# Moving the splits of the first weight slices around the conditioning, with their loads on GpSimd's queue

## The chip, the cores and the metric

One core of a Trainium2 chip. The metric is the time of one execution on the device in microseconds (us), the median of several. Engines: TensorE (PE; PEld is its weight load), VectorE (DVE), ScalarE (ACT), GpSimd (POOL) and SyncE (SP), which only issues transfers here. L461 is line 461 of the kernel.

## The reference, cut to what matters

One layer of a decoder trunk on 256 prompt positions and 8 samples with one new position each (264 columns), width 2048:

```python
mod = silu(c) @ ada_w + ada_b                      # 9 conditioning vectors, 2048 -> 6144
shift, scale, gate = split(mod, 3)
h = rmsnorm(x, g_pre) * (1.0 + scale) + shift
z = h @ w_in                                       # 2048 -> 8192: pooling, q, k, v, gates
y_a = pool_mixer(a_x) * silu(a_g)
y_b = group_norm(retention(rotary(q), rotary(k), v)) * silu(b_g)
gates = sigmoid(h @ w_merge + b_merge)             # 2048 -> 4096
out = rmsnorm((g_a * (y_a @ w_a_proj) + g_b * (y_b @ w_b_proj)) @ w_out, g_post)
y = x + gate * out
```

All in float32. h needs shift and scale, so the conditioning product comes before everything that uses h.

## The kernel before, in words

**Split products.** A float32 product is made of three faster ones. A number w is split into w_hi (w rounded to the type fp32r, by ScalarE) and w_lo = w - w_hi (by VectorE), h likewise, and TensorE adds w_hi h_hi, w_hi h_lo and w_lo h_hi (L461 to L463 for the slices, L412 to L414 elsewhere). A unit of weights is 128 x 2048 numbers; `raw` holds 3 of them, `w_hi` 3, `w_lo` 2.

**The first stage** (to about 157 us) makes h and, while it does, computes with every finished piece of h. h has 16 blocks of 128 rows, taken as 8 pairs p. For each pair:
- *the conditioning phase* (`ada_phase`, L386): 64 matmuls with 4 units of the conditioning weights, which come into `ada_ring` (8 units, so two phases);
- *the selection* (`select`, L405): ScalarE copies the phase's sums from PSUM (`ada_copy`, L698), TensorE turns them with 4 matmuls;
- *h*: VectorE has normalized the pair of x (`normalize`, L1046), and makes h from it with the selected shift and scale (`make_h`, four instructions, L1058 to L1069); ScalarE rounds it (`split_h`, L702), VectorE takes the low half (`low_h`, L1073);
- *two slices* j = 2p and 2p + 1 of the merge gates' weights, 128 x 1536 numbers each (768 KB), the part of twelve gate tiles that belongs to this pair of h. ScalarE makes the high half (`split_slice`, L681), VectorE the low half in three thirds (`split_slice(j, n)`, L1007). TensorE multiplies in three steps u (`slice_pair`, L461 to L463), each of two units of 6 matmuls: one adds up in its own bank of PSUM, the other goes to bank TV and is taken away by VectorE (`take_sum`, L1017 and L1020), which must have taken the one before.

TensorE's order is: phase 0, selection 0, then for each p from 0 to 6 the three steps of slice 2p, phase p + 1, step 0 of slice 2p + 1, selection p + 1, steps 1 and 2 of slice 2p + 1; at the end slices 14 and 15. Before slice j it waits for its low half (`lo_ready`) and, with j = 2p, for `low_h(p)`.

**The order on the other engines** is written out by hand. ScalarE (L709 on), for each p: `ada_copy(p)`, `split_slice(2p)`, `split_h(p)`, `split_slice(2p + 1)`. VectorE (L1076 on): `normalize`, `make_h`, the thirds of slice 0, `low_h`; then for p from 1 to 7 the sums of slice 2p - 2 alternating with the thirds of slice 2p - 1, `normalize(p)`, a sum, `make_h(p)`, a sum, a third of slice 2p, `low_h(p)`, a third, a sum, the last third.

**The loads** are all issued by SP, in one queue, in program order; a wait in front of one load holds all that follow. For each p: 4 conditioning units (`load_ada`, L252, waiting for a free place of the ring), then slices 2p and 2p + 1 (`load_slice`, L245; from slice 3 on each waits until slice j - 3 has been split by VectorE and so has freed its slot of `raw`).

**The next stage** is the projections of head 0. Units 0 to 2 are loaded behind the slices (L239), then trig_t (tables of the rotation, L265) and hc (L266), two more units, and behind a wait for the last sigmoid of the gates: the store of the gates to DRAM (1.5 MB, L270), cnt_t (a table of 32 KB that the pooling uses first at about 510 us, L271), s_t (L272). trig_t and cnt_t count on one semaphore; before its first rotation (L1112) VectorE waits until both are there. The split of unit 2 (L992) is behind that rotation in its order.

Of the kernel before, what the change touches and what calls it, by code (L numbers as in the profile page):

```python
# [62 lines left out]
SLICES = 16  # L63
SLICE = 6 * 256
# [14 lines left out]
def build(nc, stream, first_w, ada0, ada1, xT, x_tok, cT, vec, headc, trig, ident_in, sel_in, cnt_in, poolw, spool,  # L79
# [5 lines left out]
    with ctx:  # L85
# [3 lines left out]
        def sem(name):  # L89
            return ctx.enter_context(nc.semaphore(name))  # L90


        raw = sb("raw", [128, 3, UNIT])
# [49 lines left out]
        cnt_t = sb("cnt_t", [128, 4, 16], f32, mid)  # L143
# [36 lines left out]
        x_in = sem("x_in")  # L180
        trig_in = sem("trig_in")
        raw_loaded = [sem(f"raw_loaded{s}") for s in range(3)]
        hi_ready, lo_ready = sem("hi_ready"), sem("lo_ready")
        proj_done, taken = sem("proj_done"), sem("taken")
        ada_loaded = [sem(f"ada_loaded{s}") for s in range(8)]
# [49 lines left out]
        def _(sp):  # L235
# [2 lines left out]
                sp.wait_ge(lo_ready, SLICES + i - 2)  # L238
                sp.dma_start(raw[:, c % 3, :], stream[i]).then_inc(raw_loaded[c % 3], 16)  # L239

            def load_slice(j):
                if j >= 3:
                    sp.wait_ge(lo_ready, j - 2)
                slot = (j + 2) % 3
                sp.dma_start(raw[:, slot, 0:SLICE], first_w[j]).then_inc(raw_loaded[slot], 16)  # L245

            def load_ada(p):
                for s in range(4):
                    u = 4 * p + s
# [8 lines left out]
            sp.dma_start(sel[:, :], sel_in).then_inc(const_in, 16)  # L258
            for p in range(8):
                load_ada(p)  # L260
                load_slice(2 * p)
                load_slice(2 * p + 1)
            for c in range(3):
                load(0, c)
            sp.dma_start(trig_t[:, :, :], trig).then_inc(trig_in, 16)  # L265
            sp.dma_start(hc[:, :], headc[0]).then_inc(head_in, 16)  # L266
            load(0, 3)
            load(0, 4)
            sp.wait_ge(sig_ready, FIRST)
            sp.dma_start(gates_dram, gate_sig[:, :, :]).then_inc(gates_out, 16)  # L270
            sp.dma_start(cnt_t[:, :, :], cnt_in).then_inc(trig_in, 16)  # L271
            sp.dma_start(s_t[:, :, :], sret[0]).then_inc(state_in, 16)  # L272
            for c in range(5, 8):
                load(0, c)
# [388 lines left out]
        def _(act):  # L663
            def split(a, c, after_ya=False):

                i = 6 * a + c
                act.wait_ge(raw_loaded[c % 3], 16 * (2 * a + c // 3) + 16 + 16 * (5, 5, 6)[c % 3])
                if not isinstance(a, int):
                    act.wait_ge(proj_done, outs(a, c - 3, after_ya))
                elif i >= 3:  # L670
                    act.wait_ge(proj_done, outs(0, i - 3))
                else:
                    act.wait_ge(slice_sums, 3 * (SLICES - 3 + i) + 3)
                act.activation(w_hi[:, c % 3, :], raw[:, c % 3, :], ACT.Copy).then_inc(hi_ready, 1)  # L674

            def split_slice(j):
                slot = (j + 2) % 3
                act.wait_ge(raw_loaded[slot], 16 * (j // 3) + 16)
                if j >= 3:
                    act.wait_ge(slice_sums, 3 * (j - 3) + 3)  # L680
                act.activation(w_hi[:, slot, 0:SLICE], raw[:, slot, 0:SLICE], ACT.Copy).then_inc(hi_ready, 1)  # L681
# [12 lines left out]
            def ada_copy(p):  # L694
                act.wait_ge(ada_used, 4 * p + 4)
                if p >= 1:
                    act.wait_ge(sel_done, p)
                act.activation(part[:, :], TR[:, 0:AW], ACT.Copy).then_inc(part_ready, 1)  # L698
# [16 lines left out]
            act.wait_ge(x_ms, 1)  # L715
            act.activation(rstd[:, :], O0[:, 0:NT], ACT.Sqrt, bias=eps_t[:, :], scale=1.0 / D_MODEL).then_inc(x_std, 1)
            for p in range(8):
                ada_copy(p)
                split_slice(2 * p)
                split_h(p)  # L720
                split_slice(2 * p + 1)
            split(0, 0)
# [210 lines left out]

        @block.gpsimd
        def _(pool):
            def squares(g):
                pool.wait_ge(o_ready, 2 * g + 2)
                pool.wait_ge(o_samples, g + 1)
                pool.tensor_tensor(sq_t[:, :, :], o_t[:, :, :], o_t[:, :, :], ALU.mult).then_inc(sq_ready, 1)  # L939
                pool.wait_ge(sq_ready, g + 1)  # L940
                if not (isinstance(g, int) and g == 0):
                    pool.wait_ge(step_e, g)
                pool.tensor_tensor(osum[:, :], sq_t[:, 0, :], sq_t[:, 1, :], ALU.add).then_inc(sqs_ready, 1)

            def squares_lo(g):
                pool.wait_ge(sqhi_ready, g + 1)
                pool.tensor_tensor(osum_lo[:, :], osum[:, :], osum_hi[:, :].bitcast(f32), ALU.subtract).then_inc(sqlo_ready, 1)

            squares(0)
            squares_lo(0)  # L950
            with pool.Fori(1, H - 1) as g:
                squares(g)
                squares_lo(g)


            def windows(g):
                pool.wait_ge(taken, 50 + 4 * g)
                if g >= 1:
                    pool.wait_ge(pooled_ready, 3 * g)
                src, steps = ext, (1, 2, 4, 8)[:g + 1]  # L960
                for n, s in enumerate(steps):
                    dst = work[:, 2 * (n % 2):2 * (n % 2) + 2, :]
                    lo = 2 * s - 1
                    if n:
                        pool.wait_ge(win_step, sum(range(1, g + 1)) + n)
                    ins = pool.tensor_tensor(dst[:, :, lo:16 + TP], src[:, :, lo:16 + TP], src[:, :, lo - s:16 + TP - s], ALU.add)
                    ins.then_inc(win_step, 1)
                    src = dst

            windows(0)  # L970
            squares(H - 1)
            squares_lo(H - 1)
            for g in range(1, 4):
                windows(g)
# [3 lines left out]
        def _(dve):  # L978
# [20 lines left out]
            def split_slice(j, n):  # L999

                slot = (j + 2) % 3
                if n == 0:
                    dve.wait_ge(hi_ready, j + 1)
                    if j >= 2:
                        dve.wait_ge(slice_sums, 3 * (j - 2) + 3)
                cols = slice(512 * n, 512 * n + 512)
                sub = dve.tensor_tensor(w_lo[:, j % 2, cols], raw[:, slot, cols], w_hi[:, slot, cols].bitcast(f32), ALU.subtract)  # L1007
                if n == 2:
                    sub.then_inc(lo_ready, 1)
# [39 lines left out]
            def make_h(p):  # L1049
                dve.wait_ge(sel_done, p + 1)  # L1050
                if p == 0:
                    dve.wait_ge(bias_ready, 1)
                else:
                    dve.wait_ge(hf_ready, 4 * p)
                got = TR[:, AW:AW + 64].rearrange("p (t c) -> p t c", t=2)[:, :, 0:2 * NC]
                got = got.rearrange("p t (k n) -> p k t n", k=2)
                bias = vecs[:, V_ADAB:V_ADAB + 32].rearrange("p (k t) -> p k t", k=2)[:, :, 2 * p:2 * p + 2]
                dve.tensor_tensor(mods[:, :, :, :], got, bias.unsqueeze(3).to_broadcast([128, 2, 2, NC]), ALU.add).then_inc(mod_ready, 1)  # L1058
                dve.wait_ge(mod_ready, p + 1)
                dve.wait_ge(xn_ready, 2 * p + 2)  # L1060
                if p >= 1:
                    dve.wait_ge(h_lo_ready, p)
                    dve.wait_ge(h_hi_ready, p)
                for t in range(2):
                    dve.tensor_scalar(h_f[:, t, 0:TP], x_t[:, 2 * p + t, 0:TP], mods[:, 1, t, 0:1], mods[:, 0, t, 0:1],
                                      ALU.mult, ALU.add).then_inc(hf_ready, 1)
                dve.tensor_tensor(h_f[:, :, TP:NT], x_t[:, 2 * p:2 * p + 2, TP:NT], mods[:, 1, :, 1:NC], ALU.mult).then_inc(hf_ready, 1)
                dve.wait_ge(hf_ready, 4 * p + 3)
                dve.tensor_tensor(h_f[:, :, TP:NT], h_f[:, :, TP:NT], mods[:, 0, :, 1:NC], ALU.add).then_inc(hf_ready, 1)  # L1069
# [4 lines left out]
                                  ALU.subtract).then_inc(h_lo_ready, 1)  # L1074

            normalize(0)  # L1076
            make_h(0)
            for n in range(3):
                split_slice(0, n)
            low_h(0)  # L1080
            for p in range(1, 8):
                for n in range(3):
                    take_sum(2 * p - 2, n)
                    split_slice(2 * p - 1, n)
                normalize(p)
                take_sum(2 * p - 1, 0)
                make_h(p)
                take_sum(2 * p - 1, 1)
                split_slice(2 * p, 0)
                low_h(p)  # L1090
                split_slice(2 * p, 1)
                take_sum(2 * p - 1, 2)
                split_slice(2 * p, 2)
            for n in range(3):
                take_sum(14, n)
                split_slice(15, n)
            take_sum(15, 0)
            split(0, 0, parts=(0, 1))
            take_sum(15, 1)
# [393 lines left out]
```

## Time and profile before

| | |
|---|---|
| median of 3 runs | 969.23 us (969.15 to 970.47) |
| the profiled execution's own time | 971.4 us |
| its span | 969.6 us |
| TensorE busy | 922.6 us (95%) |
| VectorE busy | 537.0 us (55%) |
| ScalarE busy | 417.3 us (43%) |
| GpSimd busy | 54.9 us (6%) |
| granted clock of TensorE, mean | 0.987 of full speed |

How to read it: times are counted from the span's start. A row of a timeline has the start, the duration, the engine, line and operation, the tile written and those read, and in brackets how long the engine sat idle before it and what ended that. Matmuls are pipelined, so those of a run overlap; what counts is the distance between their starts.

### The profile page before, as it was taken

The numbers are of one execution on the slowest core, as the hardware profiler recorded it, in microseconds if no ns is written. First come the engines' busy times: TensorE is split into PE (matmuls) and PEld (weight loads), VectorE is DVE, ScalarE is ACT, GpSimd is POOL, SyncE is SP. The second block draws the span as 40 slices with busy tenths as digits, with TensorE's granted clock in tenths as the row PEclk, the third lists the DMA queues.
The fourth block names the chain that finished last, engine by engine and source line by source line (L and its number), as shares of the span: only waits on it lengthen the run. The fifth ranks groups of instructions, "written<-read, shape, count | busy, mean of one in ns | idle before, by whom it ended". The sixth has DMA issues, their size and how long they took to land.

```text
span 969.6 us, 18710 instructions
## 1 busy us (share of the span) xinstructions
PE 922.6 (95%) x7794; PEld 883.4 (91%) x7794; DVE 537.0 (55%) x755; ACT 417.3 (43%) x518; POOL 54.9 (6%) x38
## 2 busy tenths in 40 slices
PE   4798989899999999999999999999999999999997
PEld 1677778899999999999999999999999999999997
DVE  3555553476666766667666555445543544446664
ACT  4213135365465655645545434433533333344330
POOL 0000000001101010110103112000000000000000
PEclk9989999999999999999999999999999999999999
DMA  9998947648586585856865565567767576645535
GB/s 374 409 377 337 379 175 271 212 154 291 184 303 215 185 307 162 320 194 218 288 220 194 192 195 181 174 244 233 290 257 280 201 263 255 258 156 186 185 131 179
DMA packets 43321, 233.48 MB, mean 241 GB/s; under 512 B 9088, under 2 KB 14080, under 8 KB 17792
## 3 DMA queue, kind: packets, MB, share of 16 engines
q1 hardware_dynamic: 43264, 232.64, 66.2%
q8 instruction: 45, 0.74, 0.3%
q14 instruction: 12, 0.10, 0.0%
HBM read 218.78 MB, written 13.84 MB: 240 GB/s over the span
## 4 chain that ended last, share of the span: by engine, by line
PE 85%; DVE 8%; DMA 3%; issue 2%; ACT 1%; SPq 0%; DVEq 0%; ACTq 0%
PE bank L412 23%; PE bank L413 22%; PE bank L414 22%; PE bank L461 3%; PE bank L386 3%; DVE w_lo L992 3%; PE bank L463 2%; PE bank L462 2%; DVE s_t L1132 2%; PE bank L396 2%; DMA ada_ring<-ada 1%; DVE w_lo L1007 1%; DMA raw<-stream 1%; DMA cnt_t<-cnt_in 1%; PE bank L584 1%
## 5 line engine op out<-in xcount | busy, mean ns | idle before, releaser
L412 PE MATMUL bank<-h_hi,w_hi 128*128 128x264 f32 x1344 | 387.0, 288 | 7.7 <-DVE w_lo L992 7.5
L413 PE MATMUL bank<-h_lo,w_hi 128*128 128x264 f32 x1344 | 381.7, 284 | 0.0
L414 PE MATMUL bank<-h_hi,w_lo 128*128 128x264 f32 x1344 | 381.2, 284 | 0.0
L992 DVE TENSOR_TENSOR w_lo<-raw,w_hi 128x2048 fp32r<-128x2048 f32 x123 | 281.5, 2288 | 152.9 <-PE bank L414 146.0
L412 PEld LDWEIGHTS bank<-h_hi,w_hi 128*128 128x128 f32 x1344 | 253.9, 189 | 13.4 <-ACT work L738 6.4
L413 PEld LDWEIGHTS bank<-h_lo,w_hi 128*128 128x128 f32 x1344 | 254.1, 189 | 0.3
L414 PEld LDWEIGHTS bank<-h_hi,w_lo 128*128 128x128 f32 x1344 | 252.8, 188 | 0.0
L674 ACT ACTIVATE w_hi<-raw 128x2048 fp32r<-128x2048 f32 x124 | 237.2, 1913 | 30.7 <-PE bank L414 18.5
L461 PE MATMUL bank<-h_hi,w_hi 128*128 128x264 f32 x192 | 63.1, 329 | 18.8 <-DVE w_lo L1007 13.6
L412 PE MATMUL bank<-yb_hi,w_hi 128*128 128x264 f32 x256 | 73.2, 286 | 0.4 <-DVE w_lo L992 0.4
L412 PE MATMUL bank<-m_hi,w_hi 128*128 128x264 f32 x256 | 72.7, 284 | 0.0
L414 PE MATMUL bank<-yb_hi,w_lo 128*128 128x264 f32 x256 | 72.6, 284 | 0.0
L413 PE MATMUL bank<-m_lo,w_hi 128*128 128x264 f32 x256 | 72.5, 283 | 0.0
L414 PE MATMUL bank<-m_hi,w_lo 128*128 128x264 f32 x256 | 72.5, 283 | 0.0
L413 PE MATMUL bank<-yb_lo,w_hi 128*128 128x264 f32 x256 | 72.5, 283 | 0.0
L461 PEld LDWEIGHTS bank<-h_hi,w_hi 128*128 128x128 f32 x192 | 41.6, 217 | 23.6 <-DVE w_lo L1007 20.5
L463 PE MATMUL bank<-h_hi,w_lo 128*128 128x264 f32 x192 | 59.8, 311 | 0.0
L462 PE MATMUL bank<-h_lo,w_hi 128*128 128x264 f32 x192 | 59.5, 310 | 0.0
L412 PEld LDWEIGHTS bank<-yb_hi,w_hi 128*128 128x128 f32 x256 | 48.2, 188 | 2.6 <-issue 2.1
L939 POOL TENSOR_TENSOR sq_t<-o_t 128x528 f32<-128x528 f32 x8 | 23.5, 2942 | 443.4 <-DVE o_t L1162 443.4
L413 PEld LDWEIGHTS bank<-m_lo,w_hi 128*128 128x128 f32 x256 | 48.2, 188 | 0.0
L412 PEld LDWEIGHTS bank<-m_hi,w_hi 128*128 128x128 f32 x256 | 48.2, 188 | 0.0
(180 smaller groups left out, 1142.3 us busy)
## 6 DMA issues: line engine op xcount, KB each, us to landing
raw<-stream SPq DMA_DIRECT2D x124, 1024.0 KB, 4.9
ada_ring<-ada SPq DMA_DIRECT2D x32, 1024.0 KB, 11.6
gate_ring<-ada SPq DMA_DIRECT2D x16, 1024.0 KB, 6.5
raw<-first_w SPq DMA_DIRECT2D x16, 768.0 KB, 9.9
s_t<-sret SPq DMA_DIRECT2D x8, 1024.0 KB, 5.4
v_all<-v_dram SPq DMA_DIRECT2D x8, 1024.0 KB, 6.6
nret_s<-s_t SPq DMA_DIRECT2D x8, 1024.0 KB, 8.2
x_t<-xT SPq DMA_DIRECT2D x1, 2112.0 KB, 7.7
```

The source lines that it names most:

```text
L386: mm = pe.matmul(TR[32 * j:32 * j + 32, 0:AW], cpad[:, 8 * (j % 2) + 2 * s + kk, :], w[:, at:at + AW], start=(s == 0 and kk == 0), stop=(s ...
L396: mm = pe.matmul(TR[32 * j:32 * j + 32, 0:AW], cpad[:, 2 * v + kk, :], w[:, at:at + AW], start=(v == 0 and kk == 0), stop=(v == 7 and kk = ...
L412: pe.matmul(out, wh[:, cols], hi[:, k, :], start=(k == 0), stop=False)
L413: pe.matmul(out, wh[:, cols], lo[:, k, :], start=False, stop=False)
L414: mm = pe.matmul(out, wl[:, cols], hi[:, k, :], start=False, stop=(k == depth - 1))
L461: pe.matmul(out, hi, h_hi[:, k, :], start=(start and t == 0), stop=False)
L462: pe.matmul(out, hi, h_lo[:, k, :], start=False, stop=False)
L463: mm = pe.matmul(out, lo, h_hi[:, k, :], start=False, stop=(stop and t == 1))
L674: act.activation(w_hi[:, c % 3, :], raw[:, c % 3, :], ACT.Copy).then_inc(hi_ready, 1)
L939: pool.tensor_tensor(sq_t[:, :, :], o_t[:, :, :], o_t[:, :, :], ALU.mult).then_inc(sq_ready, 1)
L992: dve.tensor_tensor(lo, raw[:, c % 3, :], hi.bitcast(f32), ALU.subtract).then_inc(lo_ready, 1)
L1132: ins = dve.scalar_tensor_tensor(out=state, in0=v_all[:, :, :, b].rearrange("p n t -> p t n"), scalar=qk_t[:, 1, TP + b:TP + b + 1], in1=s ...
```

## The change

The slices' loads go from SP's program to GpSimd's, with semaphores of their own. From slice 3 on each waits, as before, for the slot; slice 0 waits until the second conditioning unit has landed, slices 1 and 2 until the fourth has. On ScalarE the high half of slice 2p is made before the copy of the sums instead of behind it. On VectorE all three thirds of slice 2p stand before the sum, `make_h` and `low_h` of the pair, and the thirds of slice 2p - 1 each before the sum beside them instead of behind it. The load of cnt_t moves up behind that of trig_t.

```diff
@@ sync @@
-            def load_slice(j):
-                if j >= 3:
-                    sp.wait_ge(lo_ready, j - 2)
-                slot = (j + 2) % 3
-                sp.dma_start(raw[:, slot, 0:SLICE], first_w[j]).then_inc(raw_loaded[slot], 16)
...
             for p in range(8):
                 load_ada(p)
-                load_slice(2 * p)
-                load_slice(2 * p + 1)
             for c in range(3):
                 load(0, c)
             sp.dma_start(trig_t[:, :, :], trig).then_inc(trig_in, 16)
+            sp.dma_start(cnt_t[:, :, :], cnt_in).then_inc(trig_in, 16)
             sp.dma_start(hc[:, :], headc[0]).then_inc(head_in, 16)
             load(0, 3)
             load(0, 4)
             sp.wait_ge(sig_ready, FIRST)
             sp.dma_start(gates_dram, gate_sig[:, :, :]).then_inc(gates_out, 16)
-            sp.dma_start(cnt_t[:, :, :], cnt_in).then_inc(trig_in, 16)
@@ scalar @@
             def split_slice(j):
                 slot = (j + 2) % 3
-                act.wait_ge(raw_loaded[slot], 16 * (j // 3) + 16)
+                act.wait_ge(slice_loaded[slot], 16 * (j // 3) + 16)
...
             for p in range(8):
+                split_slice(2 * p)
                 ada_copy(p)
-                split_slice(2 * p)
                 split_h(p)
                 split_slice(2 * p + 1)
@@ gpsimd @@
+            for j in range(SLICES):
+                if j >= 3:
+                    pool.wait_ge(lo_ready, j - 2)
+                else:
+                    pool.wait_ge(ada_loaded[(1, 3, 3)[j]], 16)
+                slot = (j + 2) % 3
+                pool.dma_start(raw[:, slot, 0:SLICE], first_w[j]).then_inc(slice_loaded[slot], 16)
@@ vector @@
             normalize(0)
-            make_h(0)
             for n in range(3):
                 split_slice(0, n)
+            make_h(0)
             low_h(0)
             for p in range(1, 8):
                 for n in range(3):
+                    split_slice(2 * p - 1, n)
                     take_sum(2 * p - 2, n)
-                    split_slice(2 * p - 1, n)
                 normalize(p)
+                for n in range(3):
+                    split_slice(2 * p, n)
                 take_sum(2 * p - 1, 0)
                 make_h(p)
                 take_sum(2 * p - 1, 1)
-                split_slice(2 * p, 0)
                 low_h(p)
-                split_slice(2 * p, 1)
                 take_sum(2 * p - 1, 2)
-                split_slice(2 * p, 2)
             for n in range(3):
+                split_slice(15, n)
                 take_sum(14, n)
-                split_slice(15, n)
```

The waits of `split` on `raw_loaded` lose the constant that counted the slices.

## Rows read from the trace of the kernel before

**Rows 1.** The waits of the first 180 us: total us, times, longest

```profile
PE bank L461 <- DVE w_lo L1007: 13.6, 8, 1.9
```

**Rows 2.** Windows: busy us of each engine, granted clock, DMA share, GB/s

```profile
0.00:40.00 40.00, 20.63 (x174) 12.83 (x175) 17.21 (x41) 12.54 (x19) 0.20 (x4) 1.00 0.97 392
30.00:40.00 10.00, 10.00 (x103) 8.23 (x103) 3.90 (x8) 0.42 (x2) 0.00 (x0) 1.00 1.01 418
40.00:120.00 80.00, 71.03 (x678) 61.88 (x679) 43.27 (x100) 18.48 (x19) 0.00 (x0) 0.91 0.91 366
90.00:100.00 10.00, 8.24 (x67) 8.01 (x66) 6.02 (x15) 3.47 (x4) 0.00 (x0) 1.00 0.76 294
170.00:180.00 10.00, 6.38 (x40) 6.38 (x41) 6.80 (x9) 3.07 (x4) 0.00 (x0) 0.83 0.64 221
```

**Rows 3.** The chain that ended last: phases 1, 4, 5 and 7; start, us

```profile
35.92 3.59 PE bank L386 x64
...
86.03 3.59 PE bank L386 x64
...
101.23 3.59 PE bank L386 x64
...
134.55 3.59 PE bank L386 x64
```

**Rows 4.** TensorE's timeline: first matmuls of slices 8, 14 and 15

```profile
96.46 0.39 PE L461 MATMUL bank<-h_hi,w_hi 128*128 128x264 f32 x1 [1.76 <-DVE w_lo L1007]
...
145.00 0.39 PE L461 MATMUL bank<-h_hi,w_hi 128*128 128x264 f32 x1 [1.76 <-DVE w_lo L1007]
...
152.36 0.39 PE L461 MATMUL bank<-h_hi,w_hi 128*128 128x264 f32 x1 [1.12 <-DVE w_lo L1007]
```

**Rows 5.** VectorE's timeline between phase 7 and slice 14

```profile
139.85 0.43 DVE L1020 TENSOR_TENSOR gate_sum<-bank,gate_sum 128x264 f32<-128x264 f32 x1 [3.43 <-PE bank L463]
...
141.29 0.18 DVE L1069 TENSOR_TENSOR v_t<-v_t,mods 128x16 f32<-128x16 f32 x1
...
142.71 0.70 DVE L1073 TENSOR_TENSOR h_lo<-v_t,h_hi 128x528 fp32r<-128x528 f32 x1
...
144.27 0.68 DVE L1007 TENSOR_TENSOR w_lo<-raw,w_hi 128x512 fp32r<-128x512 f32 x1
```

**Rows 6.** ScalarE's timeline in the same stretch

```profile
138.48 1.48 ACT L681 ACTIVATE w_hi<-raw 128x1536 fp32r<-128x1536 f32 x1
141.50 0.65 ACT L702 ACTIVATE h_hi<-v_t 128x528 fp32r<-128x528 f32 x1 [1.54 <-DVE v_t L1069]
```

**Rows 7.** The waits of SP's queue in the first 180 us

```profile
SPq L245 <- DVE w_lo L1007: 99.2, 13, 17.5
```

**Rows 8.** DMA issues: KB each, us to landing; then line 245 alone

```profile
ada_ring<-ada SPq DMA_DIRECT2D x32, 1024.0 KB, 11.6
...
raw<-first_w SPq DMA_DIRECT2D x16, 768.0 KB, 9.9
...
DMA to landing us min/median/max: 4.4/9.9/27.0
```

**Rows 9.** Timelines about projection 2: SP, ScalarE, VectorE, TensorE

```profile
160.65 0.43 SPq L271 DMA_DIRECT2D cnt_t<-cnt_in  x1
...
164.19 0.38 ACT L738 ACTIVATE work<-bank 64x264 f32<-64x264 f32 x1
...
170.12 0.43 DVE L1112 SCALAR_TENSOR_TENSOR work<-work,trig_t 128x264 f32<-128x264 f32 x1 [10.34 <-DMA cnt_t<-cnt_in]
...
173.62 0.59 PE L412 MATMUL bank<-h_hi,w_hi 128*128 128x264 f32 x1 [4.47 <-DVE w_lo L992]
```

**Rows 10.** TensorE's timeline at the start: second and fourth load, slice 0

```profile
14.22 1.93 PE L386 MATMUL bank<-ada_ring,cpad 128*32 128x256 f32 x16 [0.47 <-DMA ada_ring<-ada]
...
19.20 1.94 PE L386 MATMUL bank<-ada_ring,cpad 128*32 128x256 f32 x16 [0.55 <-DMA ada_ring<-ada]
...
29.33 0.56 PE L461 MATMUL bank<-h_hi,w_hi 128*128 128x264 f32 x1 [5.14 <-DVE h_lo L1073]
```

More of the change, by code:

```diff
@@ L182, in build @@
         raw_loaded = [sem(f"raw_loaded{s}") for s in range(3)]
+        slice_loaded = [sem(f"slice_loaded{s}") for s in range(3)]
         hi_ready, lo_ready = sem("hi_ready"), sem("lo_ready")
@@ L666, in split @@
                 i = 6 * a + c
-                act.wait_ge(raw_loaded[c % 3], 16 * (2 * a + c // 3) + 16 + 16 * (5, 5, 6)[c % 3])
+                act.wait_ge(raw_loaded[c % 3], 16 * (2 * a + c // 3) + 16)
                 if not isinstance(a, int):
```

## The prediction

> **What bounds the kernel now.** TensorE is busy 95% of the span (table above), so a gain has to come from its idle time or from its clock. The list of waits up to 180 us says where it idles once it has begun: 13.6 us in 8 waits for the low halves of the slices (line 1007) [rows 1]. Outside that stage one large wait is left, 4.47 us before projection 2 of head 0 [rows 9]. The windows add the clock: 0.91 granted over 40 to 120 us, 1.00 from 90 to 100, 0.83 from 170 to 180 [rows 2]. 0.91 is a mix of the two levels, 2.4 GHz and 1.2 GHz, and TensorE falls to the lower one soon after such a wait.
>
> The starts of the conditioning phases (64 matmuls in 3.59 us) give the period of the stage [rows 3]. The phase of pair 4 starts at 86.03 and that of pair 5 at 101.23: 15.20 us, with one wait of 1.76 us [rows 4] and no fall of the clock. The six periods from 35.92 to 134.55 take 98.63 us. Their share of the eight waits is 10.7 us (13.6, less 1.76 before slice 14 and 1.12 before slice 15 [rows 4]). A period with neither wait nor low clock is thus 15.20 - 1.76 = 13.44 us, six are 80.6, and 98.6 - 10.7 - 80.6 = 7.3 us is what the low clock costs, about 1.45 in each of the five other periods.
>
> Why TensorE waits stands in VectorE's timeline, here before slice 14 [rows 5]. For 3.43 us it sits idle beside the conditioning phase, though slice 14 needs splitting. Then, after the selection, everything comes at once: a sum (139.85), the four instructions that make h (the last at 141.29), a sum, a third of the split, low_h (142.71), a third, a sum, the last third (144.27). TensorE starts the slice at 145.00 and had run out of work 1.76 us before [rows 4]. ScalarE has the same order: it splits the slice's high half (138.48) behind the copy of the conditioning's sums; its split_h ends at 142.15 [rows 6].
>
> **Part 1: the slices' splits move in front of the conditioning.** On VectorE the three thirds (0.6 us each, 1.8 in all [rows 5]) leave the stretch behind the selection and go to where the 3.43 us of idle time are. normalize precedes them, so they end about 3.0 us after the phase starts, before the sum that follows the phase. low_h is then the last thing that TensorE waits for. By row: make_h ends at 141.47, split_h at 142.15 [rows 5, 6], low_h takes 0.6 and would end at 142.8. The 24 matmuls behind the selection keep TensorE at work until 143.24 (145.00 - 1.76 [rows 4]). So low_h is 0.4 us early, and the 1.76 us wait goes altogether. The wait for slice 15 (1.12) goes the same way: its split moves ahead of the sums of slice 14 and its high half is ready by then. **Waits removed: 13.6 us.** With no wait I expect no fall of the clock, because every fall in this stage came behind one: 7.3 us and once more 1.45 for slice 14. **Clock: 8.7 us.**
>
> What hides the moved work: on ScalarE split_slice (1.48 us [rows 6]) now precedes the copy of the sums, in time that it spends waiting. It must have landed data there, about 10 us after its slot was freed. If that cover is gone, its lateness goes 1:1 into the copy, the selection and low_h, less the 0.4 us.
>
> **Part 2: the slices' loads leave SP's queue for GpSimd's.** No bytes change. SP now waits 99.2 us for VectorE in front of slice loads [rows 7], with the loads of the weights behind; these waits move to GpSimd, which has nothing else until the heads' squares. The weights of a phase are then held back only by their ring. Is there enough bandwidth for the shorter period? 32 loads of 1024 KB and 16 of 768 KB are 46.1 MB [rows 8]; x (128 x 16 x 264 numbers, 2.2 MB) and the constants make it 48.6. By 40 us 15.7 MB are in (392 GB/s), and from 30 to 40, with the DMA engines busy throughout, the rate is 418 GB/s [rows 2]; at 0.42 MB/us the other 32.9 MB are in at 118.3, with landing 119. TensorE would start the last phase at 35.9 + 2.2 (below) + 80.6 = 118.7 and end it at 122.3. So transfers are some 2.4 us early at the end. It is close: a pair needs 5.77 MB, 13.7 us at that rate, more than the 13.44 of TensorE, and only the head start covers it. I take **0** for this, and as the bad end the mean of the old stage, 366 GB/s over 40 to 120 [rows 2]: 32.9 / 0.366 = 90 us, last phase over at 131.6, 9 us later.
>
> A rule of the Trainium skill speaks against this part: DMA: Bandwidth & Descriptors, Issuing engines are not separate DMA queues, says that loads from several engines run on the same 16 DMA engines and interleave, so that a second issuer saves only issue time. By that rule the part alone brings nothing, and the sum is the same, since it books nothing to the queue.
>
> **Part 3: the start.** Today the four loads of phase 0 are ahead of slices 0 and 1 in one queue; the matmuls of its second load start at 14.22 and those of its fourth at 19.20 [rows 10]. Now slice 0 is issued when the second load has landed, at 14.2, and shares the DMA engines with the third and fourth. It is 0.79 MB; at worst all of it goes first, 1.9 us; at best nothing of it is ahead. Shared by halves it is nearly all in by the time load 4 is: I take 1.5. Then ScalarE splits slice 0 (1.48) before it copies the sums, while VectorE does the reciprocal, normalize and three splits (1.8) before make_h; split_h (0.65) is no longer covered by those splits. That adds about 0.7. Slice 0's matmuls start at 29.33 now [rows 10], so 31.5. **Cost: 2.2 us** (0.7 to 2.6). Slices 1 and 2 are issued at about 21 and needed at 31 or later. Nothing shows what an issue on GpSimd's queue costs; the nearest row is the time to landing, 4.4 to 27.0 us [rows 8], and with 10 us of lead in the steady state only its upper part hurts. The Trainium skill's same page, Anatomy of one DMA, puts the fixed cost of a load from GpSimd at some 2.0 us; by that alone the sum does not change.
>
> **Part 4: cnt_t is loaded early.** VectorE waits for both tables at one point, and sits idle 10.34 us until 170.12 for cnt_t alone [rows 9]; cnt_t's issue at 160.65 stands behind the wait for the last sigmoid and the 1.5 MB store of the gates. Moved up behind trig_t it lands some 4 us before the rotation can begin (ScalarE's last copy for it ends at 164.6 [rows 9]). Then the split of projection 2 is done at about 168, before TensorE has ended projection 1 at 169.15, and its 4.47 us wait goes, with the low clock behind it (0.83 over 170 to 180 [rows 2]), 1.45 as above. **5.9 us.** What is late next there is nothing that the old trace shows: the split of projection 3 ends a microsecond ahead of its need.
>
> **Sum.** 13.6 + 8.7 - 2.2 + 5.9 = 26.0 us. The profiled execution took 971.4 us, 2.2 more than the median of the runs, 969.23: so 945.4 for such an execution and **943.2** as a median. Behind 180 us TensorE hardly waits, so what is gained earlier reaches the end.
>
> **Rivals.**
> (a) The transfers become the bound. For it: 13.7 against 13.44 us a pair. Against: the head start. At the 366 GB/s mean, 9 us are given back, and short waits would bring back a low clock once or twice (1.45 each): 943 + 9 + 2 = 954.
> (b) A short wait stays in every period, low_h's 0.4 us being used up by something, and the clock falls all the same: 7 x 1.45 = 10 us plus about 1: 954. Against it: the period from 86.03 to 101.23 held a full wait and lost nothing, so small ones need not.
> (c) Slice 0 lands late. If GpSimd's queue got its turn only behind the six weight loads queued at 14.2 (6.3 MB, 15 us), slice 0 would be there at 31 instead of 24, and ScalarE's copy waits behind it: 7 to 8 us, 951. The Trainium skill has a rule that points this way (SBUF — State Buffer, the "DVE blocks DMA" trap): GpSimd writes the descriptors itself and is locked out while VectorE runs in a two-port mode. In rows: VectorE is busy 43.27 of the 80 us from 40 to 120 [rows 2], so an issue held up by all that it does would take about twice as long, which the 10 us of lead still cover; it hurts at the start alone.
> (d) Only part 4 works, the stalls of the slices merely moving to another instruction: 969.2 - 5.9 = 963.3. The idle 3.43 us beside each phase speak against it.
> (e) Slower. Every slice takes as long as the slowest today, 27.0 us from issue to landing [rows 8]. There are three buffers and about 3 us from landing to the freed slot, so three slices take 30 us and a pair 20. Over 7.5 pairs that is 150 against 101 us: 49 lost, 26 gained, 992. It decides from a landing of about 23 us. Against it: those 27 us are a load queued behind weights in one queue, which is what GpSimd's own queue ends.
>
> **How the numbers follow.** Forecast 0.62, (a) 0.12, (b) 0.10, (c) 0.07, (d) 0.05, (e) 0.03, no change at all 0.01. The likeliest alone runs from 940.5 (start nearly free) to 946. To leave out no more than 2 in 10 the range takes in (a), (b) and (c): 939 to 955. Within 0.2% (1.9 us), about what a measurement of this kernel can tell from no change, I put 0.01; slower 0.03; faster 0.96.
>
> **What the new profile would show.** Right: no wait of line 461 for line 1007; the starts of phases 1 to 7 about 13.4 us apart, the first at 38, the last at 118 to 119; clock 1.00 from there on; VectorE's three splits in a row beside each phase; slice 0's first matmul at 31.5; the first projection at 137; no wait for cnt_t. Wrong: line 386 waiting for its weights in the late phases (a), periods near 15 us with the clock at 0.9 (b), line 681 waiting for first_w at the start (c) or throughout (e).

## The result, and the profile after

| | before | changed |
|---|---|---|
| median | 969.61 us (4 runs) | 944.33 us (943.87 to 944.89, 4 runs) |
| the profiled execution's own time | 971.4 us | 944.89 us |
| its span | 969.6 us | 942.7 us |

The ratio is 0.9739, with a 95% interval of 0.9722 to 0.9755: 25.3 us faster, where 26.0 were forecast. The step sums go by the two profiled executions, whose spans lie 26.9 us apart.

The windows of the changed kernel, in the columns of [rows 2]:

```profile
20.00:40.00 20.00, 13.18 (x106) 10.24 (x102) 11.73 (x23) 5.74 (x6) 1.63 (x4) 0.61 1.01 419
40.00:120.00 80.00, 79.53 (x844) 68.32 (x833) 52.62 (x121) 23.04 (x24) 5.81 (x11) 1.00 1.01 416
120.00:160.00 40.00, 39.55 (x334) 38.41 (x327) 22.11 (x34) 23.06 (x31) 0.00 (x0) 1.00 0.76 278
```

Over 40 to 120 us TensorE is now busy 79.5 of 80 us at a granted clock of 1.00; it was 71.0 at 0.91 [rows 2]. The DMA engines went from a share of 0.91 to 1.01: they are busy without a gap.

The phases' starts in the chain that ended last, which answer to [rows 3] (phases 1 to 5):

```profile
37.33 3.59 PE bank L379 x64
...
50.54 3.59 PE bank L379 x64
...
63.80 3.59 PE bank L379 x64
...
77.03 3.59 PE bank L379 x64
...
90.26 3.83 PE bank L379 x64
```

The distance is 13.2 us (it was 15.2 once and 16.6 to 16.8 otherwise). The last two phases are in TensorE's timeline, with the only two waits that it has between slice 0 and the first projection:

```profile
103.60 2.80 PE L379 MATMUL bank<-ada_ring,cpad 128*32 128x256 f32 x48
106.86 1.07 PE L379 MATMUL bank<-ada_ring,cpad 128*32 128x256 f32 x16 [0.47 <-DMA ada_ring<-ada]
...
117.53 2.80 PE L379 MATMUL bank<-ada_ring,cpad 128*32 128x256 f32 x48
120.58 1.07 PE L379 MATMUL bank<-ada_ring,cpad 128*32 128x256 f32 x16 [0.26 <-DMA ada_ring<-ada]
```

The fourth part of each waits for its load, and the distances are 13.4 and 13.9 us: here the transfers have caught up. The waits for line 1007 (now 1008) [rows 4] are gone altogether. VectorE's and ScalarE's timelines between phase 7 and slice 14, which answer to [rows 5] and [rows 6]:

```profile
118.79 1.89 DVE L1008 TENSOR_TENSOR w_lo<-raw,w_hi 128x512 fp32r<-128x512 f32 x3
123.37 0.43 DVE L1021 TENSOR_TENSOR gate_sum<-bank,gate_sum 128x264 f32<-128x264 f32 x1 [2.69 <-PE bank L456]
...
125.69 0.71 DVE L1074 TENSOR_TENSOR h_lo<-v_t,h_hi 128x528 fp32r<-128x528 f32 x1
```

```profile
113.69 1.49 ACT L674 ACTIVATE w_hi<-raw 128x1536 fp32r<-128x1536 f32 x1 [0.39 <-DMA raw<-first_w]
121.72 0.38 ACT L691 ACTIVATE part<-bank 128x256 f32<-128x256 f32 x1 [6.54 <-PE bank L379]
125.02 0.65 ACT L695 ACTIVATE h_hi<-v_t 128x528 fp32r<-128x528 f32 x1 [2.91 <-DVE v_t L1070]
```

The three thirds are done at 120.7, beside the phase. Between the last instruction of make_h (124.81) and low_h stands nothing but a sum, and low_h is the last thing that TensorE needs. ScalarE had waited 0.39 us for the slice's data, with 6.5 us to spare behind it.

The start, answering to [rows 10], in TensorE's timeline:

```profile
19.27 1.93 PE L379 MATMUL bank<-ada_ring,cpad 128*32 128x256 f32 x16 [1.66 <-DMA ada_ring<-ada]
...
30.24 0.56 PE L454 MATMUL bank<-h_hi,w_hi 128*128 128x264 f32 x1 [4.15 <-DVE h_lo L1074]
```

And the transfers by issue, with the time to landing, answering to [rows 8]:

```profile
ada_ring<-ada SPq DMA_DIRECT2D x32, 1024.0 KB, 22.7
...
raw<-first_w POOLq DMA_DIRECT2D x16, 768.0 KB, 10.3
```

The weights' loads take twice as long from issue to landing as before (11.6), because they are issued as soon as the ring has room and queue up (SP's waits are now for TensorE to free a place of the ring, 79.0 us in 24); the slices' take about as long as before (9.9).

### The profile page after: what moved, and what is told of

The parts are those of the page before. It is cut to its first block, busy times and chain, and to the rows that moved or that the text cites. A ratio compares the mean times of both kernels' runs of the same rounds, so it can differ in the third digit from the quotient of the medians.

```text
span 942.7 us, 18688 instructions
## 1 busy us (share of the span) xinstructions
PE 910.5 (97%) x7794; PEld 873.2 (93%) x7794; DVE 538.6 (57%) x755; ACT 417.6 (44%) x518; POOL 63.6 (7%) x54
## 4 chain that ended last, share of the span: by engine, by line
PE 86%; DVE 6%; DMA 5%; ACT 1%; issue 1%; SPq 0%; DVEq 0%; ACTq 0%
PE bank L405 24%; PE bank L406 23%; PE bank L407 23%; DMA ada_ring<-ada 4%; PE bank L454 2%; PE bank L379 2%; DVE w_lo L993 2%; PE bank L455 2%; PE bank L456 2%; DVE s_t L1132 2%; PE bank L389 2%; DMA raw<-stream 1%; PE bank L577 1%; PE bank L515 1%; PE bank L540 1%
## 5 line engine op out<-in xcount | busy, mean ns | idle before, releaser
L405 PE MATMUL bank<-h_hi,w_hi 128*128 128x264 f32 x1344 | 386.1, 287 | 3.2 <-DVE w_lo L993 3.0
L406 PE MATMUL bank<-h_lo,w_hi 128*128 128x264 f32 x1344 | 381.0, 283 | 0.0
L407 PE MATMUL bank<-h_hi,w_lo 128*128 128x264 f32 x1344 | 380.5, 283 | 0.0
L405 PEld LDWEIGHTS bank<-h_hi,w_hi 128*128 128x128 f32 x1344 | 253.2, 188 | 8.7 <-ACT work L731 6.4
L454 PE MATMUL bank<-h_hi,w_hi 128*128 128x264 f32 x192 | 59.1, 308 | 4.1 <-DVE h_lo L1074 4.1
L455 PE MATMUL bank<-h_lo,w_hi 128*128 128x264 f32 x192 | 55.7, 290 | 0.0
L456 PE MATMUL bank<-h_hi,w_lo 128*128 128x264 f32 x192 | 55.6, 289 | 0.0
L406 PEld LDWEIGHTS bank<-yb_lo,w_hi 128*128 128x128 f32 x256 | 48.2, 188 | 0.0
L407 PEld LDWEIGHTS bank<-yb_hi,w_lo 128*128 128x128 f32 x256 | 48.1, 188 | 0.0
## 6 DMA issues: line engine op xcount, KB each, us to landing
ada_ring<-ada SPq DMA_DIRECT2D x32, 1024.0 KB, 22.7
```

What stands on the lines that cost most here:

```text
L405: pe.matmul(out, wh[:, cols], hi[:, k, :], start=(k == 0), stop=False)
L406: pe.matmul(out, wh[:, cols], lo[:, k, :], start=False, stop=False)
L407: mm = pe.matmul(out, wl[:, cols], hi[:, k, :], start=False, stop=(k == depth - 1))
L454: pe.matmul(out, hi, h_hi[:, k, :], start=(start and t == 0), stop=False)
L455: pe.matmul(out, hi, h_lo[:, k, :], start=False, stop=False)
L456: mm = pe.matmul(out, lo, h_hi[:, k, :], start=False, stop=(stop and t == 1))
```

## The experiments

Every kernel ran beside the kernel before on the same chip; since the chips differ by a microsecond or so, ratios stand beside the medians. Two medians are compared directly only where both kernels ran on one chip, unless the text says otherwise. Diffs are against the changed kernel unless said otherwise.

**Part 4 alone** (against the kernel before)

```diff
             sp.dma_start(trig_t[:, :, :], trig).then_inc(trig_in, 16)
+            sp.dma_start(cnt_t[:, :, :], cnt_in).then_inc(trig_in, 16)
...
             sp.dma_start(gates_dram, gate_sig[:, :, :]).then_inc(gates_out, 16)
-            sp.dma_start(cnt_t[:, :, :], cnt_in).then_inc(trig_in, 16)
```

> The kernel before with part 4 alone: cnt_t's load behind that of trig_t. My theory: the wait of projection 2 (4.47 us) and the low clock behind it go, 5.9 us in all: about 963.6 us. Rival: the head's first rotations are held by something else that arrives as late (the state or the 1.5 MB store in the same queue), and a new wait takes over: 967 to 969.6.

Measured: 963.75 us, and 971.08 for the kernel before on that chip, ratio 0.9927 (0.9906 to 0.9948), that is 7.1 us with an interval of 5.0 to 9.1. The spans of the two profiled executions, 969.6 and 963.4, differ by 6.2. The first stage is the same to 0.1 us (first projection at 157.31, before 157.30), TensorE has no wait left from there to 180 us and its windows show why the gain is larger than the wait of 4.47:

```profile
160.00:180.00 20.00, 20.00 (x168) 20.00 (x167) 9.20 (x10) 9.59 (x11) 0.00 (x0) 1.00 0.92 340
```

It was busy 15.5 of these 20 us at a clock of 0.91 before. No other wait took over; the rival falls.

**All but part 4**

> The changed kernel with cnt_t's load back behind the store of the gates. If the parts add up, 944.3 + 5.7 = 950.0 us, with the 4.5 us wait for the split of projection 2 there again. Rival: since the first stage now ends earlier against the transfers, the wait is longer or shorter than before; then 947 or 952.

The diff is the one above, undone. Measured: 951.39 us, ratio 0.9803 (0.9783 to 0.9823); its span is 948.6, 5.9 above the changed kernel's. The wait is back in TensorE's timeline:

```profile
152.11 0.59 PE L405 MATMUL bank<-h_hi,w_hi 128*128 128x264 f32 x1 [4.36 <-DVE w_lo L993]
```

The parts add up: with or without the rest, part 4 is worth some 6 us.

**The queue alone**: GpSimd issues the slices, but ScalarE, VectorE and cnt_t keep the order of before.

```diff
             for p in range(8):
-                split_slice(2 * p)
                 ada_copy(p)
+                split_slice(2 * p)
                 split_h(p)
```

(and the loop of VectorE and the place of cnt_t likewise.)

> The changed kernel's loads (slices issued by GpSimd) with the old order on ScalarE and VectorE, and cnt_t at its old place. My theory and the Trainium skill's rule agree: no bytes change and no engine waited for a slice before, so 969.6 us within 1. The start may move, since slice 0 no longer stands behind the four loads of weights: slices 0 and 1 are now wanted before they have landed (22.99 us for slice 0, 26.7 for slice 1), which would cost 0.5 to 3 us. Rival: the queue itself frees something, 965 or less.

Measured: 972.31 us against 971.08, ratio 1.0008 (0.9994 to 1.0023). No gain, and no loss that can be told. Slice 0 starts at 29.75 (29.33 before), TensorE waits 1.76 us before each even slice as before, and the low clock is there too (0.91 over 40 to 120). The queue by itself frees nothing.

**The new order in one queue**: the slices' loads go back to SP.

```diff
@@ sync @@
+            def load_slice(j):
+                if j >= 3:
+                    sp.wait_ge(lo_ready, j - 2)
+                slot = (j + 2) % 3
+                sp.dma_start(raw[:, slot, 0:SLICE], first_w[j]).then_inc(slice_loaded[slot], 16)
...
                 load_ada(p)
+                load_slice(2 * p)
+                load_slice(2 * p + 1)
@@ gpsimd @@
-            for j in range(SLICES):
...
```

> The changed kernel with the slices' loads back in SP's queue, in the order of before (four weight units, two slices). Theory A, the rule that a second queue brings nothing: 944.3 us within 1. Theory B: in one queue a slice lands only when the weights queued ahead of it have, and the transfers run some 20 us behind their issue in the changed kernel (22.7 us from issue to landing for the weights) where the new order wants slice 2p about 11 us after its slot was freed; then ScalarE waits for first_w in every period, the copy of the sums waits behind it, and the period is longer by 1 to 3 us: 951 to 965.

Measured: 942.49 us, ratio 0.9713 (0.9692 to 0.9733). Both theories miss: it is faster than the changed kernel. Theory B had its mechanism, but at no price. The waits of the first 180 us of this kernel:

```profile
ACT w_hi L682 <- DMA raw<-first_w: 37.0, 6, 7.1
```

ScalarE does wait for slices, 37 us in all and up to 7.1, against 4.4 us in the changed kernel; but there it had some 6.5 us of idle time beside a phase, and behind these waits TensorE lost only 0.57 us in the whole stage (three waits of 0.16 to 0.24).

**The one-queue kernel and the changed kernel on one chip**

> The changed kernel, unaltered, beside the one-queue version on one chip: 0.974 of the kernel before. If GpSimd's queue costs what the two traces suggest (slice 0 shares with the loads of phase 0: TensorE's first slice at 30.2 instead of 29.4 us; the last phases end at 121.6 instead of 120.1), it is 1.5 to 2.5 us slower than the one-queue version. Rival: the difference was one of chips, and the two are within 0.5 us.

> The one-queue version again, for the comparison on one chip. Theory A2: with one queue the weights of the last phases stand ahead of slices 14 and 15, which are wanted later, so phase 7 ends sooner although the bytes are the same; and phase 0 has its loads undisturbed: 1.5 to 2.5 us faster than the changed kernel. Rival: within 0.5 us of it.

Measured on one chip: changed kernel 944.69 us (944.0 to 944.87), one queue 942.66 us (942.14 to 943.38). The ranges do not touch: **the second queue costs 2.0 us**. The one-queue kernel's phases 6 and 7, in TensorE's timeline:

```profile
103.60 3.66 PE L387 MATMUL bank<-ada_ring,cpad 128*32 128x256 f32 x64
...
116.85 3.66 PE L387 MATMUL bank<-ada_ring,cpad 128*32 128x256 f32 x64
```

No part of a phase waits for its load, 13.25 us lie between them, and phase 7 ends at 120.4, while the changed kernel beside it ended it at 121.7 with waits of 0.53, 0.35 and 0.29 us in phases 5, 6 and 7. The rate is the same in both (417 and 416 GB/s over 40 to 120 us). What differs is the order of the bytes: the weights land 16.5 us after issue in the one queue and 23.2 in the two, the slices 13.2 and 10.5. The second queue buys the slices speed that ScalarE does not need, and takes it from the loads that TensorE waits for. That is half of theory A2. The slack is not endless, though: in the one-queue kernel ScalarE's wait for the even slices grows from period to period (3.98, 4.50, 5.09, 5.65 and 6.16 us for slices 6 to 14), and its idle time before the copy of the sums shrinks from 2.48 to 0.31 us. The stage ends just in time. The other half of theory A2, the start, is not borne out by these two traces: slice 0 started at 30.22 in the one-queue kernel and at 29.64 in the other (29.35 and 30.24 in the pair of traces before), so the start varies between executions by more than it differs between the kernels. What varies is shown below, with the half loads.

**The old order for pair 0**, in the changed kernel and in the one-queue kernel

```diff
             for p in range(8):
+                if p == 0:
+                    ada_copy(p)
                 split_slice(2 * p)
-                ada_copy(p)
+                if p > 0:
+                    ada_copy(p)
...
+            make_h(0)
             for n in range(3):
                 split_slice(0, n)
-            make_h(0)
             low_h(0)
```

> The changed kernel with the old order for pair 0 alone (copy of the sums before the split of slice 0 on ScalarE, make_h before the thirds of slice 0 on VectorE). There is no idle stretch beside phase 0 to fill, so the new order only puts 0.7 us more on the path to the first slice: expected 0.5 to 1.0 us faster than the changed kernel if the first stage is bound by TensorE. Rival: the stage is bound by its transfers, which end at the same time whatever the start does (phase 7 waits 0.3 us for its last load already): then no gain.

> One queue and the old order for pair 0 together. If the start counts, 0.5 to 1.0 us faster than the one-queue version, the fastest of all; if the transfers bound the stage, the same as the one-queue version, with more waits in the last phases.

Measured, beside the two above: 944.33 us (943.97 to 945.24) and 942.37 us (942.15 to 942.49). Neither can be told from its parent, although slice 0 began at 28.46 and 27.95 us. In the first, TensorE's timeline shows where the start went:

```profile
34.40 3.96 PE L379 MATMUL bank<-ada_ring,cpad 128*32 128x256 f32 x64
47.91 2.80 PE L379 MATMUL bank<-ada_ring,cpad 128*32 128x256 f32 x48
51.71 1.07 PE L379 MATMUL bank<-ada_ring,cpad 128*32 128x256 f32 x16 [1.00 <-DMA ada_ring<-ada]
...
103.68 2.80 PE L379 MATMUL bank<-ada_ring,cpad 128*32 128x256 f32 x48
106.98 1.07 PE L379 MATMUL bank<-ada_ring,cpad 128*32 128x256 f32 x16 [0.50 <-DMA ada_ring<-ada]
...
117.64 2.80 PE L379 MATMUL bank<-ada_ring,cpad 128*32 128x256 f32 x48
```

Phase 1 begins 2.3 us sooner than in the changed kernel's companion trace (36.67), every phase from the second on waits for its last load, and phase 7 begins at 117.64, where it began at 117.58 in that companion. Phases 2 to 7 lie 13.95 us apart on average: (117.64 - 47.91) / 5. The stage ends when the bytes are in.

The one-queue kernel shows the same limit in another place than I expected. No late phase waits for its load; the slices are late instead. ScalarE waits 49.2 us for them, in seven waits, TensorE has six waits of 0.16 to 0.18 us for low_h, and phases 2 to 7 lie 13.6 to 14.0 us apart. Phase 7 begins at 116.32, where it began at 116.85 in its companion: of a start that is 2.3 us sooner (slice 0 at 27.95 against 30.22) 0.5 us are left.

**Half of the slices' bytes**

```diff
-                pool.dma_start(raw[:, slot, 0:SLICE], first_w[j]).then_inc(slice_loaded[slot], 16)
+                width = SLICE if j < 3 else SLICE // 2
+                pool.dma_start(raw[:, slot, 0:width], first_w[j][:, 0:width]).then_inc(slice_loaded[slot], 16)
```

> The changed kernel, but slices 3 to 15 load only half of their columns; the other half of each slot keeps older numbers, so the gates' sums are computed from those. 5.1 MB less to load, 12 us of transfer. If the transfers hold the last phases, phases 5 to 7 start 13.23 us apart like the others, no load is waited for there, and the time is 1.0 to 1.5 us less than the changed kernel's 944.3: 943. Rival: those waits come from the queues and not from the bytes, then no gain.

> The same half loads, with the old order for pair 0. With full loads that order made the first slice start 1.2 to 1.8 us sooner and brought nothing, since each later phase then waited for its last load (13.7 us apart). If the transfers were the reason, the earlier start now reaches the end: phase 7 at 113.8 instead of 117.6 us, about 940.5 us. Rival: the start is lost to something else, 943.

Measured: 942.48 us (ratio 0.9714, 0.9689 to 0.9739) and 941.57 us (0.9699, 0.9674 to 0.9724), on one chip. In the first, no load is waited for from slice 0 on, all phases lie 13.2 us apart, phase 7 begins at 115.96 us and the first projection at 134.06. The trace of the changed kernel that began like it (phase 1 at 36.67, here at 36.59) has them at 117.58 and 136.17: with fewer bytes 2 us come back, so these are what the transfers hold there. In the trace shown above (phase 1 at 37.26) the first projection starts at 136.06, and as it began 0.7 us later, the transfers hold 1.3 to 1.4 us of it.

In the second, phase 7 begins another 0.7 us sooner, at 115.25, and that time reaches the end (0.9 us in the medians, with overlapping ranges). It does not come from slice 0, which began at 29.89 (29.86 in the first), but from its matmuls, which came to their full rate 1.7 us sooner. I had expected phase 7 at 113.8, from a slice 0 at 28.46 as in the kernel with full loads. The traces show where these 1.4 us are. First TensorE with full loads and the old order for pair 0, then with half loads and the same order, each time at the last load of phase 0 and at slice 0:

```profile
19.73 1.07 PE L379 MATMUL bank<-ada_ring,cpad 128*32 128x256 f32 x16 [1.43 <-DMA ada_ring<-ada]
...
28.46 0.56 PE L454 MATMUL bank<-h_hi,w_hi 128*128 128x264 f32 x1 [5.56 <-DVE h_lo L1077]
```

```profile
19.75 1.94 PE L379 MATMUL bank<-ada_ring,cpad 128*32 128x256 f32 x16 [1.90 <-DMA ada_ring<-ada]
...
29.89 0.56 PE L454 MATMUL bank<-h_hi,w_hi 128*128 128x264 f32 x1 [5.14 <-DVE h_lo L1078]
```

The same 16 matmuls take 1.07 us in one execution and 1.94 in the other. Behind them TensorE adds up the squares for the norm, and ScalarE takes the root of that at 21.48 and at 22.90; everything up to slice 0 follows. From the start of these 16 matmuls to slice 0 it is 8.7 us at the fast rate and 10.1 at the slow one with the old order for pair 0, and 10.2 to 10.5 and 11.0 us with the new order in two queues. So most of the microsecond by which starts differ is the rate of TensorE in phase 0. Why it is the one in some executions and the other in the rest, no trace shows.

**A third, and two thirds, back behind low_h**

```diff
                 normalize(p)
-                for n in range(3):
+                for n in range(2):
                     split_slice(2 * p, n)
                 take_sum(2 * p - 1, 0)
                 make_h(p)
                 take_sum(2 * p - 1, 1)
                 low_h(p)
+                split_slice(2 * p, 2)
```

(with two thirds: range(1), and `split_slice(2 * p, 1)` as well.)

> The changed kernel with the last third of slice 2p's split put back behind low_h (pairs 1 to 7). low_h was 0.4 us early and a third takes 0.6, so TensorE waits 0.2 to 0.3 us before each even slice. Theory: a wait that short doesn't bring the low clock; the stage is also held by its transfers, so that only part of 7 x 0.25 us shows: 944.3 + 0.5 to 1.8. Rival (b) of the prediction: the clock falls behind any wait: 10 us more, 955.

> The same with two of the three thirds behind low_h: waits of 0.8 to 0.9 us before each even slice, half of the 1.76 us of before. Without a fall of the clock: 7 x 0.85 = 6 us less the 1.3 us that the transfers had taken anyway, 949. With the fall of the kernel before (1.45 us each): 959. The granted clock over 40 to 120 us tells the two apart: 1.00 or 0.91.

Measured: 946.15 us (0.9748, 0.9724 to 0.9773) and 951.19 us (0.9802, 0.9778 to 0.9827). The first and the last of TensorE's seven waits before the even slices in the kernel with two thirds late, and then its window over 40 to 120 us:

```profile
46.14 0.39 PE L454 MATMUL bank<-h_hi,w_hi 128*128 128x264 f32 x1 [0.92 <-DVE w_lo L1008]
...
132.29 0.39 PE L454 MATMUL bank<-h_hi,w_hi 128*128 128x264 f32 x1 [0.89 <-DVE w_lo L1008]
```

```profile
40.00:120.00 80.00, 74.54 (x761) 64.28 (x758) 48.78 (x113) 23.25 (x24) 5.80 (x11) 1.00 0.98 404
```

Seven waits of 0.9 us and the granted clock stays at 1.00 in this execution, over 120 to 140 us too. In the kernel before, seven waits of 1.76 to 1.92 us had it fall behind six of them, and the one of 1.12 before slice 15 did not [rows 4]; here its windows around slices 14 and 15:

```profile
144.00:152.00 8.00, 6.24 (x36) 6.03 (x36) 3.73 (x9) 4.71 (x6) 0.00 (x0) 0.79 0.41 131
152.00:160.00 8.00, 7.45 (x58) 7.24 (x59) 5.96 (x7) 5.86 (x11) 0.00 (x0) 1.00 0.74 244
```

The traced execution with two thirds late was the fastest of its four (949.54 us). The other three took 951.1 to 951.7: one fall of 1.45 us in each can't be excluded, seven can. The median is 2.2 us above the 949 expected, part of it because a wait costs more than its idle time, as follows. With one third the waits are 0.28 to 0.31 us, 2.1 in all, as the prediction's margin says: 0.6 of work put behind 0.3 to 0.4 of slack. Its median, 946.15, is at the upper end of what was expected (944.8 to 946.1). Rival (b) falls. A second thing can be read from the distances of the phases: 14.35 us with waits of 0.91, 13.75 with waits of 0.30, 13.23 with none. A wait costs about 0.2 us more than the idle time that the row gives. Most of this is how a row counts: idle time runs from the end of the last matmul, which lasts 0.28 us, while without a wait the next one would have started 0.12 us after it.

## Why the prediction was right, point by point

**The waits.** Forecast 13.6 us removed, all of it; so it is. The stretch behind the selection was cleared as worked out, and low_h has the slack that was read from [rows 5] and [rows 6]: the experiment with one third back used it up and 0.3 us more.

**The period was mis-sized by 0.2 us.** The step was "a period with neither wait nor low clock is thus 15.20 - 1.76 = 13.44". Measured 13.23. The difference is what a wait costs beside its idle time, and what the two experiments show again (14.35 - 0.91 = 13.44 and 13.75 - 0.30 = 13.45). Over 8 waits, 1.6 us more than forecast.

**The clock.** Forecast 8.7 us and a granted clock of 1.00 from there on; the windows have 1.00 over 40 to 160. The step "every fall in this stage came behind a wait" held; that a wait must bring a fall would not have held, and the prediction had not claimed it for short ones: at 0.9 us there was none. The clock's 8.7 us are thus gained, all or nearly all, even by a version that removes only half of each wait: the one with two thirds late has waits of 6.4 us in seven, and is some 6.5 us slower than the changed kernel (951.19 against 944.69 us, on two chips), not the 16 that seven falls would make it.

**The start.** Forecast 2.2 us, of which 1.5 for the fourth load of phase 0 sharing with slice 0. In the trace the last matmuls of phase 0 begin 5.23 us behind those of the second load (19.27 - 14.04), before 4.98 (19.20 - 14.22): that term was 0.25. The new order was put at 0.7: from the last matmuls of phase 0 to slice 0 it is 11.0 us with the new order and 10.1 with the old one at the same slow rate, 0.8 us. Slice 0 landed at 23.2 and made ScalarE wait 0.34 us. TensorE's first slice came 0.9 us later than before, phase 1 1.4 us later (37.33 against 35.92), as more of slice 0 ran at the low clock: its matmuls lay 0.22 us apart up to 35.4 us, 5.2 us long, against 4.1 before. The granted clock is no guide here: it stands at 1.00 over the first 40 us of the kernel before [rows 2], where slice 0's matmuls started 0.22 us apart too. As the rate in phase 0 moves the start by a microsecond between executions, the size of the whole term is known no better than that. In the changed kernel it hardly counts: the transfers set the end of the stage.

**The transfers.** The step was "transfers are some 2.4 us early at the end", price 0, from 48.6 MB, 15.7 in by 40 us and 0.42 MB/us after: all in at 119. Bytes and rate were nearly right (416 GB/s), and the phases are 13.7 us apart or more where the transfers set them, as 5.77 MB at that rate say. The margin was wrong from both sides. TensorE was early: the period had been taken too long (6 x 0.2 = 1.3 us up to phase 7) and the start too late (0.8), so that without a wait it would have wanted its last weights at about 119.4 and not at 121.4. And these came at 120.58, 1.6 us later than computed: 0.8 of it is the rate (32.9 MB at 416 instead of 420 GB/s), and the first load of the next stage, issued at 117.17, shares the DMA engines by then. Slices 14 and 15 came ahead of phase 7's weights, which the one queue turns round. So 1.4 us (this trace) to 2 us (the half-bytes kernel against its like) of rival (a) came true, in a term that was put at 0. It is the sum's one negative surprise, and that it cancels the positive one of the period is luck.

**The queue.** Forecast at nothing, with the rule of the Trainium skill (DMA: Bandwidth & Descriptors, Issuing engines are not separate DMA queues) pointing the same way. The queue alone measures 1.0008 (0.9994 to 1.0023), so rule and trace agree there. Where the transfers bind, the forecast of nothing was short of the truth: the rate is the same with one queue and with two (417 and 416 GB/s), but the choice of queue decides whose bytes come first, and here it was the wrong ones, 2.0 us. Nothing of rival (c) was seen: slices landed 8.5 to 12.7 us after issue throughout. The descriptor trap that the Trainium skill describes (SBUF — State Buffer, the "DVE blocks DMA" trap) did not show with VectorE busy 52.6 of 80 us: an issue on GpSimd took 0.53 us, at the first 0.72. No run shows in which mode VectorE's instructions ran, and the rule is for a two-port mode, so this is no test of it.

**Part 4.** Forecast 5.9 us: 6.2 in the spans with part 4 alone, 5.9 with it undone.

**The sum at the first projection.** It began at 157.30 and now begins at 136.06: 21.2 us, forecast 20.1 (22.3 less 2.2). The waits' extra cost gave 1.6 more (8 x 0.2) and the start 0.8 more, the transfers took some 1.4 in the last phases (0.2 and 0.7 in the distances of 13.4 and 13.9 us, 0.5 in phase 7 itself, which ends at 121.65): 21.1. With part 4 that is 26.9 in the spans; the medians have 25.3, as the execution profiled before was itself 1.8 us above its median.

**What stays open.** Why TensorE runs the end of phase 0 and much of slice 0 at half its rate in some executions and not in others. Beyond the forecast, the version with one queue beats the changed kernel by 2.0 us, at 0.9714 (0.9699 to 0.9728) of the kernel before; with the old order for pair 0 added it has 0.9709 (0.9695 to 0.9723), no different.

## What to carry to other kernels

Work that waits for nothing but data loaded long ago belongs where its engine idles beside another engine's long phase, not in the chain that follows the phase. When the chain has been cleared, ask at once what the transfers allow: add up the bytes of the stage and set them against the shortened time, for there the next bound stands. And where the DMA engines are never idle, as here, a second queue added no speed (416 against 417 GB/s) and only changed whose bytes came first: give that to the loads that the bound engine waits for, and leave late the ones that have slack.

## What the runs showed of the hardware

- The low clock is not the price of any wait: seven waits of 0.9 us, 14.35 us apart, left the granted clock at 1.00 over 40 to 120 us in the traced execution. In the kernel before, seven of 1.76 to 1.92 us brought falls behind six of them and the clock to 0.91, and one of 1.12 us brought none.
- A wait of TensorE costs about 0.2 us beyond the idle time of its row: periods of 13.23, 13.75 and 14.35 us with waits of 0, 0.30 and 0.91.
- The same work at the start can run at either of two rates from one execution to the next: the last 16 matmuls of phase 0 took 1.07 or 1.94 us, and slice 0 came 8.7 or 10.1 us after their start.
- A load in a queue of its own is held up little by the other queue's backlog: 768 KB issued on GpSimd's queue landed in 8.5 to 12.7 us, while 1024 KB loads on SP's took 22.7 (median) to 30.8 us, both at a DMA share of 1.01.
